# Where the weight ring and the activation buffers start in on-chip memory, modulo 256 bytes

## The chip, the cores and the metric

The kernel runs on one core of one Trainium2 chip. The metric is the device time of one launch in microseconds. The kernel before takes 2471.91 us, the median of 3 runs (2470.83 to 2474.18).

## The reference

A two-layer decoder trunk in float32 over 256 tokens with a model width of 2048. Cut to what matters:

```python
h = x                                         # (1, 256, 2048)
for i in range(2):
    xn = rmsnorm(h, g_mix[i])
    mix = attn_mixer(xn, ...) if i == 0 else rglru_mixer(xn, ...)   # projections 2048 -> 5656 / 4096, and back
    h = h + mix
    h = h + swiglu(rmsnorm(h, g_ffn[i]), wg, wu, wd)                # 2048 -> 2 x 5632 -> 2048
    gate = sigmoid(rmsnorm(h, g_ple[i]) @ w_ple_gate[i])            # 2048 -> 2048
    h = h + gate * (p[i] @ w_ple_proj[i])                           # 256 -> 2048
return rmsnorm(h, g_final)
```

Nearly all of the arithmetic is in these dense products of a (256 x K) activation with a (K x N) weight. There are about 443 MB of weights, and each is read once.

## The kernel before, in words

**Precision by splitting.** Every dense product is made of three products in the fast 32-bit matmul format. A weight is split into `w_hi` (the value rounded by a ScalarE copy, line 537) and `w_lo` (the rest, by VectorE, line 774). An activation is split into `x_hi` and `x_lo` in the same way. The product is `x_hi*w_hi + x_hi*w_lo + x_lo*w_hi`, on lines 1276, 1277 and 1278, all three into one PSUM accumulator.

**Slots.** The weights come in pieces of 2 k-tiles x 512 columns (512 KB), one DMA each, issued by SyncE. A piece is called a slot here. The ring has four places (`NRING = 4`): `raw` takes the DMA, `w_hi` and `w_lo` the two halves. Slot number t uses place t modulo 4. The whole program goes through 820 slots in one fixed order, phase after phase. TensorE does 12 matmuls for a slot: for each of 2 token tiles and each of 2 k-tiles the three products. In each of them the activation (128 x 128) is the stationary operand, which a weight load brings into the array, and the weight piece (128 x 512) is the moving operand. While one matmul streams its 512 columns, the weight load for the next matmul runs beside it. (Four slots are an exception, for the 24 gate columns: there the operands change roles.)

**Order.** Each engine runs its own list of instructions in an order fixed when the program is written; they meet through semaphores. ScalarE and VectorE prepare slot t+1 and later while TensorE multiplies slot t, as far as the ring lets them. Between slots TensorE does the transposes of results (line 1232) and, in the attention and recurrence phases, small plain float32 matmuls.

**Buffers.** The activations stand in three pairs of buffers, each with a `hi` and a `lo` part of [k-tiles, 256 tokens] in 4-byte elements: A (`xa_hi`, `xa_lo`, 16 k-tiles) feeds both products of the feed-forward block and the gate of the layer's end; B (`xb_hi`, `xb_lo`, 16 k-tiles) feeds the input and output projections of the mixers; H (`hid_hi`, `hid_lo`, 44 k-tiles) feeds the down projection and lies over B. A fourth pair, `pT_hi` and `pT_lo`, feeds one slot in nine of the last phase of each layer. One k-tile takes 1024 bytes per partition, and the second token tile begins 512 bytes behind the first, so every stationary operand of a buffer has the same start modulo 256. The same holds for the weights: the second k-tile in a place begins 2048 bytes behind the first.

**Addresses.** All buffers are laid out by hand, one behind the other from byte 16512 of the partition (`put`), and some at computed offsets (`at`). The distance of two ring places is `WROW * 4` bytes. From these lines follow the starts, modulo 256, in the table of the section on the change.

Of the kernel before, what the change touches and what calls it, by code (L numbers as in the profile page):

```python
# [27 lines left out]
F32R = mybir.dt.float32r  # L28
# [7 lines left out]
S = NT * P  # L36
D = 2048
KD = D // P
DFF = 5632
KF = DFF // P  # L40
CW = 512
# [16 lines left out]
LRU_C = 8.0  # L58
NBLK = 8
XPAD = 260  # L60
WROW = 2 * CW + 32


class Kind:
# [164 lines left out]
def trunk(nc, x, p, g_mix, g_ffn, g_ple, g_final, w_in_attn, cmp_pe_k, cmp_w1_k, cmp_w2_k,  # L229
# [6 lines left out]
    with ctx:  # L236

        base = (nc.sbuf_base + 63) // 64 * 64
        size = nc.sbuf_usable_end - 64 - base
        ctx.enter_context(nc.sbuf_tensor("slab", [P, size - 64], mybir.dt.uint8))  # L240
        top = [base]

        def at(name, shape, dt, offset):
            return nc.alloc_sbuf_tensor_at(name, [P, *shape], dt, offset=offset)

        def put(name, shape, dt=F32):
            n = int(np.prod(shape)) * (2 if dt == BF16 else 4)
            t = at(name, shape, dt, top[0])
            top[0] += (n + 31) // 32 * 32
            return t  # L250

        h = put("h", [NT, D])
        raw = put("raw", [NRING, 2 * CW])
        w_hi = put("w_hi", [NRING, WROW], F32R)
        w_lo = put("w_lo", [NRING, WROW], F32R)
        stage = put("stage", [NT, CW])
# [20 lines left out]
        ssqb = put("ssqb", [NT, HEADS])  # L277
        rstdb = put("rstdb", [NT, HEADS])
        sp_t = put("sp_t", [6, KD])
        a_off = top[0]  # L280
        big = a_off + 2 * KD * S * 4
        s_off = big + 2 * KD * S * 4
        assert big + 2 * KF * S * 4 <= base + size - 64, (big + 2 * KF * S * 4, base + size)
        X = {"A": (at("xa_hi", [KD, S], F32R, a_off), at("xa_lo", [KD, S], F32R, a_off + KD * S * 4)),
             "B": (at("xb_hi", [KD, S], F32R, big), at("xb_lo", [KD, S], F32R, big + KD * S * 4)),
             "H": (at("hid_hi", [KF, S], F32R, big), at("hid_lo", [KF, S], F32R, big + KF * S * 4))}

        vrow = at("vrow", [3, P], F32, s_off + 28672)
        gmix = at("gmix", [P], F32, s_off + 28672 + 3 * P * 4)
# [1278 lines left out]
```

How the kernel before makes its waits and increments, by code:

```python
            def load_slot(q, i, r, j):  # L423
                t = slot_no(q, i, r, j)
                s = ring_place(t, j)
                k0, nk, c0, w = slot_shape(q, r, j)
                if not (isinstance(t, int) and t < NRING):
                    sp.wait_ge(lo_ready, t - (NRING - 1))
                col = q.cols[r] + c0 + i * (CW if q.loop else 2 * CW)
                weight = q.weight[r].replace("gate", "proj") if is_proj(q, j) else q.weight[r]
                src = W[weight][:, k0:k0 + nk, bass.ds(col, w)]
                dst = raw[:, s, 0:nk * w].rearrange("p (k n) -> p k n", k=nk)
                sp.dma_start(dst, src).then_inc(raw_in[s], 16)
# [1 line left out]
            def load_vectors():  # L435
                sp.wait_ge(vrow_clear, 1)
                for dst, src in ((vrow[32:64, 0], g_ffn.rearrange("a (k p) -> (a k) p", p=P)),
                                 (vrow[64:96, 0], g_ple.rearrange("a (k p) -> (a k) p", p=P)),
                                 (vrow[96:104, 0], diff_subln[0]),
# [9 lines left out]
            def run_chunk(q, i, r, prev):  # L449
# [13 lines left out]
                        sp.dma_start(lam_in[:, n, :], v[0].partition_broadcast(P)).then_inc(lam_in_sem, 16)  # L463
                if q.name == "gkvc" and r == 1:
                    sp.wait_ge(vec_turned, 2)
                    sp.dma_start(w1[1][:], cmp_w1_v[0].rearrange("l d e -> d l e")).then_inc(w1_in[1], 16)
                if q.name == "out0" and i == 0 and r == 1:
                    sp.wait_ge(scored, 32)
                    for layer in range(2):
```

## Time and profile before

| what | value |
|---|---|
| time, median of 3 runs | 2471.91 us (2470.83 to 2474.18) |
| the profiled execution: its own time, and its span | 2473.23 us, 2471.5 us |
| mean granted TensorE clock | 0.997 |
| TensorE matmuls, busy | 2445.6 us, 99% |
| VectorE, ScalarE busy | 53%, 46% |
| DMA | 443.87 MB, 180 GB/s on average |

The span is from the first to the last instruction. The profiled execution's own time is 1.7 us longer than its span and 1.3 us longer than the median of the timed runs. The busy time of one matmul contains the passage through the array, which overlaps the next matmul's, so the cost of a matmul is not its duration (about 393 ns) but the distance from its start to the start of the next. That distance is read from the timeline, whose starts are given to 0.01 us; over a slot of 12 matmuls the rounding is below 1 ns for each.

### The profile page before, as it was taken

The page shows a single profiled execution, that of the slowest core. Times are in us where ns is not written, and L with a number is a line of the kernel's source. Part 1 is how long each engine was busy: PE and PEld are TensorE (multiplying, and loading weights), DVE is VectorE, ACT ScalarE, POOL GpSimd, SP SyncE. Part 2 cuts the span into 40 slices and gives each one's busy share as a digit, 9 for nine tenths or more (in the row PEclk, how much of TensorE's full clock was granted, in tenths as well). Part 3 has the DMA queues.
Part 4 walks back from the last instruction along what each step waited for, and adds up shares of the span by engine and source line. Part 5 has one row for each costly group of instructions (what it writes and reads, how often), then busy time and mean ns, then how long its engine had stood idle before and what let it go on. Part 6 is the DMA issues. An engine that isn't in the chain of part 4 may idle for free.

```text
span 2471.5 us, 29756 instructions
## 1 busy us (share of the span) xinstructions
PE 2445.6 (99%) x11084; PEld 1994.7 (81%) x11084; DVE 1315.4 (53%) x1677; ACT 1139.5 (46%) x1533; POOL 3.2 (0%) x17
## 2 busy tenths in 40 slices
PE   8999999999999999999999999999999999999997
PEld 7888778888888888888888888888888888888886
DVE  5545665555454454444566676554454454444455
ACT  5435555544444444444454575544444444344454
POOL 0000000000000000000000000000000000000000
PEclk9999999999999999999999999999999999999999
DMA  7744435666666665555557445566666666555563
GB/s 215 229 120 120 131 117 182 185 187 186 187 187 182 186 186 184 187 188 187 187 187 235 140 154 178 186 183 185 187 187 184 186 183 188 186 187 187 187 204 135
DMA packets 234042, 443.87 MB, mean 180 GB/s; under 512 B 16184, under 2 KB 21344, under 8 KB 233824
## 3 DMA queue, kind: packets, MB, share of 16 engines
q1 hardware_dynamic: 233904, 442.62, 58.7%
q8 instruction: 60, 0.98, 0.2%
q14 instruction: 30, 0.25, 0.0%
q10 hardware_dynamic: 48, 0.02, 0.0%
HBM read 440.49 MB, written 2.10 MB: 179 GB/s over the span
## 4 chain that ended last, share of the span: by engine, by line
PE 96%; DVE 1%; ACT 1%; DMA 1%; issue 0%; ACTq 0%; DVEq 0%
PE ps L1278 30%; PE ps L1276 30%; PE ps L1277 30%; PE ps L1232 2%; PE ps L1487 1%; PE ps L1400 1%; PE ps L1331 1%; DMA raw<-in_w_in_rec_dram 1%; DVE w_lo L774 0%; ACT w_hi L537 0%; PE ps L1412 0%; PE ps L1437 0%; ACT prob L691 0%; DMA h<-in_x_dram 0%; PE ps L1371 0%
## 5 line engine op out<-in xcount | busy, mean ns | idle before, releaser
L774 DVE TENSOR_TENSOR w_lo<-raw,w_hi 128x1024 fp32r<-128x1024 f32 x820 | 998.4, 1220 | 1071.1 <-ACT w_hi L537 1070.1
L537 ACT ACTIVATE w_hi<-raw 128x1024 fp32r<-128x1024 f32 x820 | 863.1, 1055 | 1137.3 <-PE ps L1278 1108.2
L1278 PE MATMUL ps<-w_hi,xa_lo 128*128 128x512 f32 x1664 | 656.9, 395 | 0.0
L1277 PE MATMUL ps<-w_lo,xa_hi 128*128 128x512 f32 x1664 | 654.2, 393 | 0.0
L1276 PE MATMUL ps<-w_hi,xa_hi 128*128 128x512 f32 x1664 | 653.9, 393 | 0.0
L1277 PEld LDWEIGHTS ps<-w_lo,xa_hi 128*128 128x128 f32 x1664 | 312.7, 188 | 73.1
L1276 PEld LDWEIGHTS ps<-w_hi,xa_hi 128*128 128x128 f32 x1664 | 312.6, 188 | 70.5
L1278 PEld LDWEIGHTS ps<-w_hi,xa_lo 128*128 128x128 f32 x1664 | 312.6, 188 | 68.8
L1276 PE MATMUL ps<-w_hi,xb_hi 128*128 128x512 f32 x864 | 351.3, 407 | 3.9 <-DVE xb_lo L837 2.3
L1278 PE MATMUL ps<-w_hi,xb_lo 128*128 128x512 f32 x864 | 341.9, 396 | 0.0
L1277 PE MATMUL ps<-w_lo,xb_hi 128*128 128x512 f32 x864 | 341.0, 395 | 0.0
L1278 PE MATMUL ps<-w_hi,hid_lo 128*128 128x512 f32 x704 | 277.9, 395 | 0.0
L1277 PE MATMUL ps<-w_lo,hid_hi 128*128 128x512 f32 x704 | 276.8, 393 | 0.0
L1276 PE MATMUL ps<-w_hi,hid_hi 128*128 128x512 f32 x704 | 276.3, 392 | 0.0
L1276 PEld LDWEIGHTS ps<-w_hi,xb_hi 128*128 128x128 f32 x864 | 163.2, 189 | 43.5 <-issue 4.5
L1278 PEld LDWEIGHTS ps<-w_hi,xb_lo 128*128 128x128 f32 x864 | 163.2, 189 | 37.0
L1277 PEld LDWEIGHTS ps<-w_lo,xb_hi 128*128 128x128 f32 x864 | 163.3, 189 | 35.1
L1277 PEld LDWEIGHTS ps<-w_lo,hid_hi 128*128 128x128 f32 x704 | 132.3, 188 | 31.1
L1276 PEld LDWEIGHTS ps<-w_hi,hid_hi 128*128 128x128 f32 x704 | 132.3, 188 | 30.0
L1278 PEld LDWEIGHTS ps<-w_hi,hid_lo 128*128 128x128 f32 x704 | 132.3, 188 | 29.1
L691 ACT ACTIVATE prob<-prob,nmax 128x128 f32<-128x128 f32 (+1 forms) x64 | 28.6, 448 | 56.0 <-DVE nmax L1058 56.0
L1232 PEld LDWEIGHTS ps<-ident,stage 128*128 128x128 f32 x304 | 35.5, 140 | 5.1
(200 smaller groups left out, 1043.9 us busy)
## 6 DMA issues: line engine op xcount, KB each, us to landing
raw<-in_w_ffn_gate_dram SPq DMA_DIRECT2D x176, 512.0 KB, 3.6
raw<-in_w_ffn_up_dram SPq DMA_DIRECT2D x176, 512.0 KB, 3.6
raw<-in_w_ffn_down_dram SPq DMA_DIRECT2D x176, 512.0 KB, 3.6
raw<-in_w_in_attn_dram SPq DMA_DIRECT2D x88, 512.0 KB, 3.7
raw<-in_w_ple_gate_dram SPq DMA_DIRECT2D x64, 512.0 KB, 3.8
raw<-in_w_in_rec_dram SPq DMA_DIRECT2D x64, 512.0 KB, 4.3
raw<-in_w_out_attn_dram SPq DMA_DIRECT2D x32, 512.0 KB, 3.7
raw<-in_w_out_rec_dram SPq DMA_DIRECT2D x32, 512.0 KB, 3.7
```

The costliest lines, as they stand in the source:

```text
L537: nc.scalar.activation(w_hi[:, s, 0:n], raw[:, s, 0:n], ACT.Copy).then_inc(hi_ready, 1)
L691: ins = nc.scalar.activation(pr, pr, ACT.Exp, scale=-1.0, bias=nmax[:, u % 2, n:n + 1], accum_out=esum[:, u % 2, n:n + 1])
L774: nc.vector.tensor_tensor(w_lo[:, s, 0:n], raw[:, s, 0:n], w_hi[:, s, 0:n].bitcast(F32), ALU.subtract).then_inc(lo_ready, 1)
L1232: ins = nc.tensor.transpose(o, src(m, f), ident[:])
L1276: nc.tensor.matmul(o, xh[:, k, tok], w_hi[:, s, wk], start=(k == 0), stop=False)
L1277: nc.tensor.matmul(o, xh[:, k, tok], w_lo[:, s, wk], start=False, stop=False)
L1278: ins = nc.tensor.matmul(o, xl[:, k, tok], w_hi[:, s, wk], start=False, stop=(k == nkt - 1))
L1331: ins = nc.tensor.matmul(ps[:, EX + kind, 0:2 * NCMP].rearrange("p (g n) -> p g n", g=2), w1[kind][:, l], x30, start=(l == 0), stop=(l == ...
L1400: ins = nc.tensor.matmul(ps[:, EX, cols], q_t[:, m * P:(m + 1) * P], k_t[:, 0:(m + 1) * P], start=True, stop=True)
L1487: ins = nc.tensor.matmul(ps[:, EX + g, e * S:(e + 1) * S], lru_w[:, g, n, k, e * P:(e + 1) * P], xc[:, 2 * n + k], start=(k == 0), stop=(k ...
```

## The change

It changes addresses and nothing else: the instructions of every engine, their order and their waits are the same. The distance of two ring places goes from 4224 to 4160 bytes (padding of 128 bytes to 64), the ring and buffer A are rounded up to a multiple of 256, B begins 32 bytes later, H where B would begin without these 32, and `hid_lo` leaves 128 bytes free behind `hid_hi`.

```diff
-WROW = 2 * CW + 32
+WROW = 2 * CW + 16
@@
         raw = put("raw", [NRING, 2 * CW])
+        top[0] = (top[0] + 255) // 256 * 256
         w_hi = put("w_hi", [NRING, WROW], F32R)
         w_lo = put("w_lo", [NRING, WROW], F32R)
@@
-        a_off = top[0]
-        big = a_off + 2 * KD * S * 4
+        a_off = (top[0] + 255) // 256 * 256
+        big = a_off + 2 * KD * S * 4 + 32
+        hid_off = big - 32
         s_off = big + 2 * KD * S * 4
-        assert big + 2 * KF * S * 4 <= base + size - 64, (big + 2 * KF * S * 4, base + size)
+        assert hid_off + 2 * KF * S * 4 + 128 <= base + size - 64, (hid_off + 2 * KF * S * 4, base + size)
         X = {"A": (at("xa_hi", [KD, S], F32R, a_off), at("xa_lo", [KD, S], F32R, a_off + KD * S * 4)),
              "B": (at("xb_hi", [KD, S], F32R, big), at("xb_lo", [KD, S], F32R, big + KD * S * 4)),
-             "H": (at("hid_hi", [KF, S], F32R, big), at("hid_lo", [KF, S], F32R, big + KF * S * 4))}
+             "H": (at("hid_hi", [KF, S], F32R, hid_off), at("hid_lo", [KF, S], F32R, hid_off + KF * S * 4 + 128))}
```

Starts modulo 256 bytes, worked out from the code:

| buffer | role in the 512-column matmuls | before | after |
|---|---|---|---|
| `w_hi`, `w_lo`, places 0, 1, 2, 3 | moving | 128, 0, 128, 0 | 0, 64, 128, 192 |
| `xa_hi`, `xa_lo` | stationary | 192, 192 | 0, 0 |
| `xb_hi`, `xb_lo` | stationary | 192, 192 | 32, 32 |
| `hid_hi`, `hid_lo` | stationary | 192, 192 | 0, 128 |
| `pT_hi`, `pT_lo` | stationary | 128, 128 | 0, 0 |
| `raw`, `h` | source of the split; residual | 128, 128 | 128, 128 |
| `stage`, `sg`, `ident` | results, identity for transposes | 128 | 0 |
| small tensors of the attention and the recurrence | | 192, 128 | 32, 0 |

## Rows read from the trace of the kernel before

**Rows 1.** The page, busy time (share of the span) and number of instructions.

```profile
PE 2445.6 (99%) x11084; PEld 1994.7 (81%) x11084; DVE 1315.4 (53%) x1677; ACT 1139.5 (46%) x1533; POOL 3.2 (0%) x17
```

**Rows 2.** The page, the span in 40 slices: TensorE busy and its granted clock.

```profile
PE   8999999999999999999999999999999999999997
PEclk9999999999999999999999999999999999999999
```

**Rows 3.** The page, costliest groups: busy us, mean ns; idle before, releaser.

```profile
L774 DVE TENSOR_TENSOR w_lo<-raw,w_hi 128x1024 fp32r<-128x1024 f32 x820 | 998.4, 1220 | 1071.1 <-ACT w_hi L537 1070.1
L537 ACT ACTIVATE w_hi<-raw 128x1024 fp32r<-128x1024 f32 x820 | 863.1, 1055 | 1137.3 <-PE ps L1278 1108.2
L1278 PE MATMUL ps<-w_hi,xa_lo 128*128 128x512 f32 x1664 | 656.9, 395 | 0.0
...
L1278 PE MATMUL ps<-w_hi,xb_lo 128*128 128x512 f32 x864 | 341.9, 396 | 0.0
...
L1278 PE MATMUL ps<-w_hi,hid_lo 128*128 128x512 f32 x704 | 277.9, 395 | 0.0
```

**Rows 4.** Waits of TensorE: us in total, times, longest.

```profile
PE ps L1494 <- DMA gmix<-in_g_mix_dram: 3.2, 1, 3.2
PE ps L1232 <- DVE xb_lo L837: 2.5, 1, 2.5
PE ps L1276 <- DVE xb_lo L837: 2.3, 1, 2.3
...
PE ps L1276 <- DVE w_lo L774: 0.6, 1, 0.6
```

**Rows 5.** Timeline of TensorE, down projection: an even slot, then an odd one.

```profile
1141.58 0.39 PE L1276 MATMUL ps<-w_hi,hid_hi 128*128 128x512 f32 x1
...
1142.04 0.40 PE L1278 MATMUL ps<-w_hi,hid_lo 128*128 128x512 f32 x1
...
1144.37 0.39 PE L1276 MATMUL ps<-w_hi,hid_hi 128*128 128x512 f32 x1
1144.60 0.39 PE L1277 MATMUL ps<-w_lo,hid_hi 128*128 128x512 f32 x1
...
1147.12 0.39 PE L1276 MATMUL ps<-w_hi,hid_hi 128*128 128x512 f32 x1
```

**Rows 6.** Timeline of TensorE, an even slot with `pT` stationary.

```profile
2380.75 0.39 PE L1276 MATMUL ps<-w_hi,pT_hi 128*128 128x512 f32 x1
...
2381.91 0.39 PE L1278 MATMUL ps<-w_hi,pT_lo 128*128 128x512 f32 x1
...
2383.49 0.39 PE L1276 MATMUL ps<-w_hi,xa_hi 128*128 128x512 f32 x1
```

**Rows 7.** Timeline of TensorE, an odd slot with `pT` stationary.

```profile
2405.65 0.39 PE L1276 MATMUL ps<-w_hi,pT_hi 128*128 128x512 f32 x1
2405.88 0.40 PE L1277 MATMUL ps<-w_lo,pT_hi 128*128 128x512 f32 x1
...
2408.45 0.39 PE L1276 MATMUL ps<-w_hi,xa_hi 128*128 128x512 f32 x1
```

**Rows 8.** The chain of waits in order of time, from 1368 us: start, us.

```profile
1368.60 3.45 PE ps L1487 x16
```

**Rows 9.** Instructions on `pT_hi`, and line 1232 by operand: ns min/median/max.

```profile
L1276 PE MATMUL ps<-w_hi,pT_hi x32: 389/392/398, 1226.5 to 2457.6; 128*128 128x512 f32 x32
...
L1232 PE MATMUL ps<-ident,stage x304: 271/273/275, 48.8 to 2122.2; 128*128 128x128 f32 x152
...
L1232 PE MATMUL ps<-ident,o_all x32: 270/272/273, 356.3 to 380.4; 128*128 128x128 f32 x32
```

## The prediction

> **What bounds the kernel now.** I read the page's busy times first: TensorE is busy for 99% of the span, VectorE for 53%, ScalarE for 46% [rows 1], and the slices show the granted clock at 2.4 GHz practically throughout, with no gap on TensorE behind the first slice [rows 2]. Then the waits of TensorE: the longest are 3.2, 2.5 and 2.3 us, once each, and weights that come late cost it 0.6 us in the whole run [rows 4]. ScalarE and VectorE are the ones that wait: 1108 us of ScalarE's idle time ahead of the splits ends with TensorE's release of a ring place, and VectorE waits for ScalarE [rows 3]. So the kernel's time is a number of matmuls by the distance of their starts. The dense ones, three lines with equal counts, are 3 x (1664 + 864 + 704) = 9696 [rows 3], and 3 x 32 = 96 with `pT` [rows 9], 9792 together.
>
> **The spacing depends on the place in the ring.** In the down projection an even slot takes from 1141.58 to 1144.37, 2.79 us for 12 matmuls or 232.5 ns each; the next, odd one takes until 1147.12, 2.75 us or 229.2 ns [rows 5]. Both do the same work on the same engine with nothing late. What differs is the address: the weights start at 128 modulo 256 in even places and at 0 in odd ones, the activations at 192 in both. The slots that multiply `pT` change the other operand, to 128. There the even slot takes 2.74 us, 228.3 ns each, and its last seven 1.58 us, 225.7 ns [rows 6]; the odd one takes 2.80 us, 233.3 ns [rows 7]. So even places take longer with activations at 192 and less with activations at 128. The place alone doesn't decide it, nor the activation alone; the simplest reading is that the distance of the moving operand's start from the stationary operand's, modulo 256, does, while a weight load runs beside the matmul.
>
> I call that distance the offset (weight start minus activation start, modulo 256). The trace then has one value for each of four:
> - offset 0: 228.3 ns over the whole slot; 225.7 once it has settled, seven matmuls [rows 6];
> - offset 64 (odd places now): 229.2; settled, 2.52 us for eleven, 229.1 [rows 5];
> - offset 128: 233.3; settled, 2.57 us for eleven, 233.6 [rows 7];
> - offset 192 (even places now): 232.5; settled, 2.33 us for ten, 233.0 [rows 5].
>
> The kernel now runs at offsets 64 and 192 by turns: (229.2 + 232.5)/2 = 230.85 ns whole, 231.05 settled. 9792 x 230.85 = 2260 us of the 2473.2 us of the profiled execution.
>
> The Trainium skill speaks against any effect: its page "TensorE: Matmul & The Clock Gate", section "Step-by-step: what each phase is for", says that TensorE has two independent read ports into SBUF and that loading the next weights takes no bandwidth from the running matmul. By that rule addresses don't matter and the change is worth nothing (it is the second rival below). The trace doesn't bear it out, with 229.2 against 232.5 ns in neighbouring slots.
>
> **The change, part by part.**
>
> *Buffer A, 3 x 1664 = 4992 matmuls.* With A at 0 and the places at 0, 64, 128 and 192, all four offsets come once in four slots. Whole slots: (228.3 + 229.2 + 233.3 + 232.5)/4 = 230.8, a change of 0.0 ns. Settled: (225.7 + 229.1 + 233.6 + 233.0)/4 = 230.35, a change of -0.7 ns. The truth depends on how long the low value at offset 0 takes to settle: in the `pT` slot it took five matmuls, but there the stationary base changed as well. The step from place 3 to place 0 is there after the change too, so some of it will be paid. I take -0.5 ns, nearer to the settled value, since nine of ten matmuls of the three other kinds of slot are settled ones. 4992 x -0.5 = -2.5 us.
>
> *Buffer H, 3 x 704 = 2112.* `hid_hi` at 0 and `hid_lo` at 128: two of three weight loads see the offset of the place, one that plus 128. Over four places each offset still comes equally often, so if the costs add, the mean is A's: 2112 x -0.5 = -1.1 us. Whether a mixed sequence settles at all is not in the trace; its bounds are the lowest and highest settled values, 225.7 and 233.6, so -5.3 to +2.6 ns against the present mean of 231.0: -11.2 to +5.5 us.
>
> *Buffer B, 3 x 864 = 2592.* At 32 the offsets become 224, 32, 96 and 160, halfway between those seen. No row shows one. Interpolating between neighbours gives the mean again, 2592 x -0.5 = -1.3 us, which I take. Bounds from the slots: 225.7 and 233.6, so -13.7 to +6.7 us. The rows farther off are the small matmuls of the recurrence, 16 of 256 columns in 3.45 us, 215.6 ns each, with both operands in 4-byte elements [rows 8]: if they are what a matmul costs without any disturbance and B came free of it, (215.6 - 231.0) x 2592 = -40 us. In the other direction, if a start off the 64-byte grid cost one more step of the size between offsets 0 and 128 (233.6 - 225.7 = 7.9 ns), it is +20.5 us.
>
> The Trainium skill's "SBUF — State Buffer", section "Specifications (TRN2)", gives 16-byte lines in SBUF; 32 is a multiple of that, so by this page a start at 32 touches no more lines than one at 0 and the +20.5 us would not arise. No run here shows the size of a line.
>
> *`pT`, 96 matmuls.* It now meets all offsets: nothing.
>
> *The splits.* ScalarE's copy takes 1055 ns and VectorE's subtraction 1220 ns per slot of about 2.77 us [rows 3]; both have over half of each slot to spare, so even 10% on either for a new address would stay hidden, and its cover is gone only beyond 2.7 us. *Transposes:* 273 ns with a source at 128 and 272 with one at 192 [rows 9]; they don't feel the address, 0. *The small matmuls* of attention and recurrence move from 192 to 32 or 0; they are about 200 us of the run together with the transposes, and 215.6 ns apart where their operands both stand at 192 [rows 8]; 0, at most a us or two either way.
>
> *Sum:* -2.5 - 1.1 - 1.3 = -4.9 us. From the profiled execution's 2473.2 that is 2468.3; the timed runs have their median 1.3 us lower, so 2467.0. If TensorE gets through a slot quicker, nothing is late next, as the splits have the slack just named and raw weights arrive well ahead.
>
> **The rivals.**
>
> *B and H land on the quick side.* The four values are not symmetric around a middle, and the states are plainly sequences that lock into a rhythm: 225.7 settled against 228.3 with the entry. An activation 32 bytes off may lock into the quick one in all places. Then B gains 5.3 ns: 2592 x -5.3 = -13.7, with -3.6 from A and H, -17.3: 2454.6 us. If H does the same, 2444.5. For it: the low value exists. Against it: it has been seen at one offset only.
>
> *Addresses shift the pattern, not the mean.* The disturbances are only moved about, and the entry into the low value eats its gain, as in the whole-slot values (0.0 ns): 2471.9 us. This is also what the skill's rule on the two read ports would give. For it: whole slots sum to 230.8 against 230.85. Against it: the `pT` slot's settled 225.7.
>
> *Slower: the 32-byte start of B.* If every weight load from B reaches over one more piece of memory and this delays the streaming weights by one step, B's matmuls rise by 7.9 ns: +20.5 - 3.6 = +16.9, 2488.8 us. It decides against the change as soon as B loses more than 3.6/2592 = 1.4 ns per matmul. For it: every start in the dense part is a multiple of 64 now, and half of those slots already take 232.5 ns. Against it: nothing in the rows shows the load as the limit. A milder form is that offset isn't the rule and 0 against 0 is a costly pairing; all at 233.6 would be 9792 x 2.6 = +25 us.
>
> **How the numbers follow.** What a measurement of this kernel can tell from no change is about 0.2%, 4.9 us. Forecast (offset rule), 0.38: its centre lies on that border, so 0.20 faster and 0.18 same; its own range 2461 to 2472. Quick side: 0.25, faster. Pattern only: 0.12, same. Slower: 0.25. That gives faster 0.45, same 0.30, slower 0.25. The range 2450 to 2482 holds the forecast, the second rival, most of B's quick side and the milder half of the slower one, and leaves out about 0.08 below and 0.11 above.
>
> **What would show it.** In the timeline after, the slots of the feed-forward phases in places 0, 1, 2, 3 should take about 2.72 to 2.74, 2.75, 2.80 and 2.79 us. If A's slots show these four, the offset rule holds; if place 0 takes 2.8, the absolute address counts. B's slots in the projections tell the 32-byte question: all near 2.71 is the first rival, all above 2.82 the slower one. Transposes and splits should keep their durations, and TensorE's waits their few us. The prediction is wrong if A's four slots average below 2.74 or above 2.79 us, or if B leaves the band of 225.7 to 233.6 ns.

## The result, and the profile after

The changed kernel takes 2481.76 us, the median of 5 runs (2481.38 to 2482.02), against 2472.92 us for the kernel before beside it. The ratio is 1.0035 with a 95% interval of 1.0021 to 1.0049: slower by 0.35%, some 9 us. The profiled execution spans 2480.1 us, 8.6 us more than before. The time lies within the range of 2450 to 2482 us, but only 0.2 us inside its upper end, and in the direction that had a chance of 0.25.

The page says that the kind of kernel is the same. TensorE is still busy 99% of the span, and the two groups that split the weights keep their durations:

```profile
PE 2454.5 (99%) x11084; PEld 1993.5 (80%) x11084; DVE 1315.5 (53%) x1677; ACT 1138.7 (46%) x1533; POOL 3.2 (0%) x17
...
L776 DVE TENSOR_TENSOR w_lo<-raw,w_hi 128x1024 fp32r<-128x1024 f32 x820 | 998.2, 1220 | 1080.4 <-ACT w_hi L539 1077.0
L539 ACT ACTIVATE w_hi<-raw 128x1024 fp32r<-128x1024 f32 x820 | 862.1, 1054 | 1147.7 <-PE ps L1280 1128.7
```

Line numbers have moved by two. VectorE takes 1220 ns and ScalarE 1054 against 1055 [rows 3]; both idle 9 to 10 us more, because TensorE hands the ring places back later. The waits of TensorE (total us, times, longest) are again a few us, the largest at the very start:

```profile
PE ps L1496 <- DMA gmix<-in_g_mix_dram: 5.0, 1, 5.0
PE ps L1234 <- DVE xb_lo L839: 2.5, 1, 2.5
PE ps L1278 <- DVE xb_lo L839: 2.3, 1, 2.3
```

Against [rows 4] the first is 1.8 us longer, a DMA before the first matmul. The transposes (ns min/median/max) are as in [rows 9], 273 and 272 ns, though `ident` and `o_all` have moved:

```profile
L1234 PE MATMUL ps<-ident,stage x304: 270/273/273, 49.7 to 2129.0; 128*128 128x128 f32 x152
...
L1234 PE MATMUL ps<-ident,o_all x32: 270/272/273, 358.7 to 381.7; 128*128 128x128 f32 x32
```

So the time is in the distance between dense matmuls. The timeline of TensorE gives it slot by slot (12 matmuls between the rows shown). Four slots of the feed-forward phase with buffer A, places 1, 2, 3 and 0:

```profile
701.90 0.40 PE L1278 MATMUL ps<-w_hi,xa_hi 128*128 128x512 f32 x1
...
704.66 0.40 PE L1278 MATMUL ps<-w_hi,xa_hi 128*128 128x512 f32 x1
...
707.46 0.39 PE L1278 MATMUL ps<-w_hi,xa_hi 128*128 128x512 f32 x1
...
710.25 0.39 PE L1278 MATMUL ps<-w_hi,xa_hi 128*128 128x512 f32 x1
...
713.00 0.40 PE L1278 MATMUL ps<-w_hi,xa_hi 128*128 128x512 f32 x1
```

They take 2.76, 2.80, 2.79 and 2.75 us. Offset 0 is the short one and 128 and 192 are the long ones, as the offset rule had it. Now buffer B (places 0 to 3, the last row is a transpose) and buffer H (places 0 to 3):

```profile
436.77 0.40 PE L1278 MATMUL ps<-w_hi,xb_hi 128*128 128x512 f32 x1
...
439.57 0.40 PE L1278 MATMUL ps<-w_hi,xb_hi 128*128 128x512 f32 x1
...
442.37 0.40 PE L1278 MATMUL ps<-w_hi,xb_hi 128*128 128x512 f32 x1
...
445.18 0.39 PE L1278 MATMUL ps<-w_hi,xb_hi 128*128 128x512 f32 x1
...
447.98 0.27 PE L1234 MATMUL ps<-ident,h 128*128 128x128 f32 x1
...
1139.92 0.40 PE L1278 MATMUL ps<-w_hi,hid_hi 128*128 128x512 f32 x1
...
1142.72 0.39 PE L1278 MATMUL ps<-w_hi,hid_hi 128*128 128x512 f32 x1
...
1145.51 0.39 PE L1278 MATMUL ps<-w_hi,hid_hi 128*128 128x512 f32 x1
...
1148.31 0.39 PE L1278 MATMUL ps<-w_hi,hid_hi 128*128 128x512 f32 x1
...
1151.09 0.40 PE L1278 MATMUL ps<-w_hi,hid_hi 128*128 128x512 f32 x1
```

B takes 2.80 to 2.81 us in every place, H 2.78 to 2.80. No short slot is left in either, where before every other slot took 2.75 [rows 5].

The same over the whole trace: mean distance in ns from one dense matmul's start to the next, distances of 300 ns and more left out (they contain other work), about 9600 distances:

| | before | after | after, by place 0, 1, 2, 3 |
|---|---|---|---|
| A | 230.9 | 231.1 | 228.3, 230.3, 232.9, 233.0 |
| B | 231.1 | 233.4 | 233.3, 233.3, 233.5, 233.5 |
| H | 230.9 | 232.6 | 232.7, 233.0, 233.1, 231.6 |

With all distances counted, long ones too, A gives 1.2 us more, B 3.4 (its short distances alone 2.25 ns x 2465 = 5.5, its long ones 2 less), H 3.6 and `pT` nothing, 8.2 together. The other matmuls give 1.5 less and the start 1.8 more; that is the 8.6 us of the span, to rounding.

The 2 us less in B's long distances are no gain of the change. In the profiled execution of the kernel before, the granted clock fell to half, 1.2 GHz, for 3.4 us in the attention phase, behind a stretch in which TensorE was busy for 1.6 of 3.9 us; seven of B's matmuls stand 427 ns apart there. In that of the changed kernel it did not fall there. The same stretch before and after, with the granted clock in the third column from the end:

```profile
359.90:363.40 3.50, 3.50 (x10) 2.67 (x10) 2.85 (x5) 0.00 (x0) 0.00 (x0) 0.51 0.63 206
```

```profile
360.00:363.50 3.50, 1.50 (x7) 1.26 (x8) 3.50 (x6) 1.85 (x4) 0.00 (x0) 1.00 0.34 115
```

With the matmuls of the first slot, also 427 ns apart, it is 13 such distances before and 8 after, 1.0 us; one distance of 1.03 us before, behind weights that came late, makes most of the rest. So B's loss by the addresses is nearer to the 5.5 us of its short distances than to 3.4.

### The profile page after: what moved, and what is told of

The parts are those of the page before. It is cut to its first block, busy times and chain, and to the rows that moved or that the text cites. A ratio compares the mean times of both kernels' runs of the same rounds, so it can differ in the third digit from the quotient of the medians.

```text
span 2480.1 us, 29756 instructions
## 1 busy us (share of the span) xinstructions
PE 2454.5 (99%) x11084; PEld 1993.5 (80%) x11084; DVE 1315.5 (53%) x1677; ACT 1138.7 (46%) x1533; POOL 3.2 (0%) x17
## 4 chain that ended last, share of the span: by engine, by line
PE 98%; DVE 1%; ACT 0%; DMA 0%; issue 0%; ACTq 0%; DVEq 0%
PE ps L1278 31%; PE ps L1280 30%; PE ps L1279 30%; PE ps L1234 2%; PE ps L1489 1%; PE ps L1402 1%; PE ps L1333 1%; PE ps L1414 0%; PE ps L1439 0%; PE ps L1440 0%; PE ps L1441 0%; DMA h<-in_x_dram 0%; PE ps L1373 0%; PE ps L1363 0%; PE ps L1352 0%
## 5 line engine op out<-in xcount | busy, mean ns | idle before, releaser
L776 DVE TENSOR_TENSOR w_lo<-raw,w_hi 128x1024 fp32r<-128x1024 f32 x820 | 998.2, 1220 | 1080.4 <-ACT w_hi L539 1077.0
L539 ACT ACTIVATE w_hi<-raw 128x1024 fp32r<-128x1024 f32 x820 | 862.1, 1054 | 1147.7 <-PE ps L1280 1128.7
```

The lines of the kernel that those rows point to most:

```text
L539: nc.scalar.activation(w_hi[:, s, 0:n], raw[:, s, 0:n], ACT.Copy).then_inc(hi_ready, 1)
L776: nc.vector.tensor_tensor(w_lo[:, s, 0:n], raw[:, s, 0:n], w_hi[:, s, 0:n].bitcast(F32), ALU.subtract).then_inc(lo_ready, 1)
```

## The experiments

All of them build on the changed kernel. "Offset" is the start of the moving weights minus the start of the stationary activations, modulo 256 bytes. A spacing without a row is a mean over the run's trace, formed as in the table above.

**Everything at one residue** (4 runs). "Residue" is the start modulo 256. The edit against the changed kernel, cut to what matters:

```diff
-WROW = 2 * CW + 16
+WROW = 2 * CW + 0
@@
-        big = a_off + 2 * KD * S * 4 + 32
-        hid_off = big - 32
+        big = a_off - 0 + 2 * KD * S * 4 + 0
+        hid_off = a_off - 0 + 2 * KD * S * 4 + 0
```

and `hid_lo` directly behind `hid_hi`.

> All ring places, A, B, H and pT start at 0 modulo 256 (ring step 4096 bytes), so every 512-column matmul runs at offset 0 (weight start minus activation start, modulo 256). Theory 1, the offset rule: every slot settles at the low value seen in place 0 of the changed kernel, 226.7 ns instead of a mean of 232.0; 9792 x -5.3 = -52 us against the changed kernel, about 2430 us. Rival: the low value needs a change of place, or the other engines that now read and write at the same residue disturb it: spacing of 229 or more, 2455 us or more.

Measured: 2432.57 us (2432.27 to 2432.84), ratio to the kernel before 0.9838, interval 0.9822 to 0.9855. The timeline with A:

```profile
700.73 0.39 PE L1278 MATMUL ps<-w_hi,xa_hi 128*128 128x512 f32 x1
...
703.45 0.39 PE L1278 MATMUL ps<-w_hi,xa_hi 128*128 128x512 f32 x1
...
706.17 0.39 PE L1278 MATMUL ps<-w_hi,xa_hi 128*128 128x512 f32 x1
```

Each slot takes 2.72 us, 226.7 ns per matmul, in all four places; over the trace A has 226.8, H 226.7, B 227.7. The expectation of about 2430 us was met. It is a version that beats both kernels, by 40 us and 49 us, and needs less memory than either. The low value needs no change of place, and there is no sign that engines working at the same residue get into each other's way (`raw` and `h` stay at 128).

**B back at 0** (10 runs): `big` without the 32 bytes, all else as changed.

> The changed kernel with buffer B at 0 instead of 32 modulo 256; all else as changed (places at 0, 64, 128, 192). Theory 1: B's slots become like A's, 228.3, 230.3, 232.9, 233.0 by place, mean 231.1 instead of 233.4; 2592 x -2.3 = -6 us against the changed kernel, 2476 us. Rival (B is slow because it is interleaved with other work and has other neighbours, not because of the 32 bytes): B stays at 233.4, 2482 us.

Measured: 2475.10 us (2474.71 to 2477.43), 6.7 us below the changed kernel; ratio to before 1.0013 (1.0004 to 1.0023). B's mean is 231.2 ns, and B's matmuls give about 6 us of the difference. Its place 0 takes 2.74 us where it took 2.80:

```profile
433.11 0.39 PE L1278 MATMUL ps<-w_hi,xb_hi 128*128 128x512 f32 x1
...
435.85 0.40 PE L1278 MATMUL ps<-w_hi,xb_hi 128*128 128x512 f32 x1
```

A and H kept their values to 0.1 ns in every place. B's loss comes from the 32 bytes, not from its neighbours.

**`hid_lo` back at 0** (one run): without the 128 bytes between `hid_hi` and `hid_lo`.

> The changed kernel with hid_lo at 0 instead of 128 modulo 256, like hid_hi. Theory 1: H's slots become like A's, mean 231.1 instead of 232.6 (place 0 at 228.3); 2112 x -1.5 = -3 us against the changed kernel. Rival (H's cost has nothing to do with hi and lo standing apart): place 0 of H stays at 232.7.

Measured: 2478.74 us in one run, 3.0 below the changed kernel. H has A's values by place (228.6, 230.3, 232.8, 233.0), place 0:

```profile
1149.81 0.39 PE L1278 MATMUL ps<-w_hi,hid_hi 128*128 128x512 f32 x1
...
1152.55 0.40 PE L1278 MATMUL ps<-w_hi,hid_hi 128*128 128x512 f32 x1
```

That is 2.74 us against 2.80. H's matmuls give 3.0 us. The time of one run could not show as little by itself, since the runs of the kernel before lie up to 4 us apart; the spacing shows it. A's place 0 settles at 227 ns after five matmuls. In H's place 0 of the changed kernel the distances are 236, 232, 233, 236, 224, 231, 236, 235, 233, 233, 235 and 231 ns: with the offset jumping by 128 at every third weight load, twelve matmuls don't settle.

**The rotation alone** (10 runs): both edits together.

> The changed kernel with B and hid_lo both at 0: only the ring's rotation (0, 64, 128, 192) and the common start of all activations are left of the change. Theory 1: every buffer has A's values by place (228.3, 230.3, 232.9, 233.0, mean 231.1), against 230.9 before; 9792 x 0.2 = 2 us over before, 2472 to 2475 us, so B's and H's new starts account for the rest of the change's loss. Rival: B's and H's losses don't add up, and 3 us or more of the loss stay (2476 us or above).

Measured: 2473.48 us (2471.81 to 2475.01), ratio 1.0002 (0.9993 to 1.0012), no difference to the kernel before. A has 231.1, B 231.2, H 231.2 ns. The losses of B and H add up: 2481.8 - 6.7 - 3.0 = 2472.1. What is left of the change, four offsets by turns in place of two, is worth nothing that the time shows. (By the spacing, 0.1 to 0.3 ns above before, it costs up to 2 us, which is less than the runs' own spread.)

**Three odd multiples of 32** (one run): all places at 0, A at 32, B at 96, H at 160.

> All ring places at 0; A at 32 (offset 224), B at 96 (offset 160), H at 160 (offset 96). Every buffer has one offset, so settled values can be read for three odd multiples of 32. Theory 1a (a stationary start off the 64-byte grid costs by itself): all three at 233 or above. Theory 1b (the cost is a smooth function of the offset): 224 between 226.7 and 233, 96 between 229 and 233.6, 160 at about 233.

Measured: 2496.37 us. A (offset 224):

```profile
705.76 0.40 PE L1278 MATMUL ps<-w_hi,xa_hi 128*128 128x512 f32 x1
...
708.56 0.40 PE L1278 MATMUL ps<-w_hi,xa_hi 128*128 128x512 f32 x1
```

2.80 us, 233.3 ns, and the same for H at offset 96; B at 160 has 234.1. The smooth function of 1b fails at 224, which is 32 bytes from the best value and costs the full 6.6 ns; 96 and 160 it had about right. 1a fits here, but it names the wrong cause, as the next run shows.

**Both operands off the grid** (one run): places and A at 32, B at 64, H at 0.

> All ring places at 32, A at 32 (offset 0), B at 64 (offset 224), H at 0 (offset 32). Theory 1 (the offset decides, not the absolute start): A at 226.7 although both operands start off the 64-byte grid, B at 233 to 234 although its stationary operand is on the grid. Rival (a start off the 64-byte grid costs by itself): A above 230.

Measured: 2463.86 us. A, then H:

```profile
700.85 0.39 PE L1278 MATMUL ps<-w_hi,xa_hi 128*128 128x512 f32 x1
...
703.57 0.39 PE L1278 MATMUL ps<-w_hi,xa_hi 128*128 128x512 f32 x1
...
1140.44 0.40 PE L1278 MATMUL ps<-w_hi,hid_hi 128*128 128x512 f32 x1
...
1143.24 0.40 PE L1278 MATMUL ps<-w_hi,hid_hi 128*128 128x512 f32 x1
```

A: 2.72 us with both operands 32 bytes off the 64-byte grid. H: 2.80 us with its stationary operand at 0 and the weights at 32. B at offset 224 has 233.2 with its stationary operand on the grid. Theory 1a is out: at offsets 0 and 224 the offset decides, not where either operand starts.

**Finer steps** (one run each): ring steps of 4112 and of 4100 bytes, so that the places stand 16 or 4 bytes apart.

> Ring step 4112 bytes, so the places start at 0, 16, 32 and 48 modulo 256; A at 0 (offsets 0, 16, 32, 48), B at 128 (offsets 128 to 176), H at 192 (offsets 64 to 112). It reads the spacing at twelve offsets in one trace. Theory 1 (offset 0 is one of few low values, everything off the 64-byte grid costs 233): 226.7 to 228 in A's place 0, 233 in its places 1 to 3, H 229 in place 0 and 233 in 1 to 3, B 233 or more; time about 2480 us or more. Rival (a smooth valley around 0): A's place 1 lies between 226.7 and 229.

> Ring step 4100 bytes, places at 0, 4, 8 and 12 modulo 256; A at 0 (offsets 0, 4, 8, 12), B at 64 (192 to 204), H at 32 (224 to 236). Theory 1 (memory is reached in pieces larger than 12 bytes, and a start inside a piece costs one more): A at 233 in places 1 to 3 and 228 in place 0. Rival (only larger distances matter): A stays near 227 in all four places.

Measured 2481.61 and 2489.74 us. Mean distance in ns by ring place, A and H only (a slot's first matmuls still carry the place before, which can change a mean by over 1 ns: offset 0 has 228.8 behind offset 12, as shown, and 230.0 behind offset 48):

| offset | 0 | 4 | 8 | 12 | 16 | 32 | 48 | 64 | 80 | 96 | 112 | 224 | 228 | 232 | 236 |
|---|---|---|---|---|---|---|---|---|---|---|---|---|---|---|---|
| ns | 228.8 | 237.5 | 233.1 | 230.5 | 231.5 | 233.7 | 232.7 | 229.1 | 231.1 | 234.3 | 231.1 | 232.8 | 235.9 | 234.1 | 228.9 |

The worst of them was 4 bytes from the best. B, left out of the table because other work stands between its slots, has 237.8 at offset 196, again 4 bytes past a multiple of 64. These rows are A in place 1 of the second run, 2.84 us:

```profile
703.58 0.40 PE L1279 MATMUL ps<-w_hi,xa_hi 128*128 128x512 f32 x1
...
706.42 0.40 PE L1279 MATMUL ps<-w_hi,xa_hi 128*128 128x512 f32 x1
```

Theory 1 of the first run had H's place 0, A's places 2 and 3 and the time about right and missed the other places of A and H: 16, 80 and 112 lie well below 233, and so do 12 and 236 of the second run, so "off the 64-byte grid costs 233" is wrong. Its rival missed too, with 231.5 at offset 16, and both theories of the second run missed, so there is no valley around 0 either. No settled sequence was found below 226.7.

The first run also shows a limit of the offset rule. B's place 0 has offset 128 with the same starts each time, and still two different sequences. In some slots distances of 229 and 238 ns alternate, 2.80 us for twelve, 233.3 ns each (first two rows). In others a pattern of seven repeats, 1.63 us for seven, 232.4 ns each (last two rows):

```profile
411.95 0.39 PE L1279 MATMUL ps<-w_hi,xb_hi 128*128 128x512 f32 x1
...
414.75 0.39 PE L1279 MATMUL ps<-w_hi,xb_hi 128*128 128x512 f32 x1
...
1311.21 0.39 PE L1279 MATMUL ps<-w_hi,xb_hi 128*128 128x512 f32 x1
...
1312.84 0.39 PE L1280 MATMUL ps<-w_lo,xb_hi 128*128 128x512 f32 x1
```

So the offset alone doesn't fix the spacing to the last nanosecond; what ran just before seems to choose the sequence, which was not tested.

**Is it the length of the weight load?** Three runs with stationary operands of 32 columns instead of 128: for the middle product alone, on the changed kernel; for all products, at offset 0; and for all at the offsets of the scan by 32 (both times with 128 columns kept in a product's first and last k-tile). The edit of the first:

```diff
-                        nc.tensor.matmul(o, xh[:, k, tok], w_lo[:, s, wk], start=False, stop=False)
+                        nc.tensor.matmul(o[0:32], xh[:, k, m * P:m * P + 32], w_lo[:, s, wk], start=False, stop=False)
```

> The changed kernel with the x_hi*w_lo product cut to 32 stationary columns (rows 0 to 31 of the output only, the low product of the other 96 tokens of each tile is left out). The weight load for it, which runs beside the first of each three matmuls, becomes short (about 100 ns instead of 188); all matmuls still stream 512 columns. Theory 1 (the excess over about 216 ns comes from the weight load's reads beside the stream): the distance from the first matmul's start to the second's falls by 6 ns or more, the other two keep 230 to 233. Rival (the stream costs this by itself, by its own start address): all three keep their spacing.

The loads (ns min/median/max) did become short:

```profile
L1278 PEld LDWEIGHTS ps<-w_hi,xa_hi x1664: 187/188/190, 457.8 to 2453.9; 128*128 128x128 f32 x185
...
L1279 PEld LDWEIGHTS ps<-w_lo,xa_hi x1664: 107/108/112, 458.0 to 2454.1; 128*32 128x32 f32 x185
```

In A the distance beside the short load fell by 1.6 ns, from 231.2 to 229.6, where theory 1 wanted 6, and the one after the third matmul rose from 231.0 to 232.0. The means of A, B and H fell by 0.3, 1.3 and 1.7 ns. The time was 2472.48 us, 9.3 below the changed kernel.

> Everything at 0 modulo 256 (offset 0 throughout), and the three products cut to 32 stationary columns in all but the first and last k-tile (output rows 32 to 127 miss most of the sum). Weight loads take about 108 ns instead of 188, the streams keep 512 columns. Theory 2 (the excess over 216 ns grows with the reads of the weight load): the settled spacing falls from 226.7 to about 219. Rival, theory 3 (only the start of the load beside the stream counts, or a fixed cost of the stream): it stays at 226.7 within 1 ns.

> The same short loads with A at offset 224, B at 160, H at 96, where full loads settle at 233.3 ns. Theory 2: A and H fall by 6 ns or more. Theory 3: they stay at 233.3. If they fall to the spacing of the same loads at offset 0, the address only matters through the part of the load that was cut.

Measured 2473.61 and 2508.52 us. H at offset 0 with short loads, then A at offset 224 with short loads:

```profile
1142.73 0.40 PE L1280 MATMUL ps<-w_hi,hid_hi 128*32 128x512 f32 x1
...
1145.51 0.40 PE L1280 MATMUL ps<-w_hi,hid_hi 128*32 128x512 f32 x1
```

```profile
703.22 0.40 PE L1280 MATMUL ps<-w_hi,xa_hi 128*32 128x512 f32 x1
...
706.10 0.40 PE L1280 MATMUL ps<-w_hi,xa_hi 128*32 128x512 f32 x1
```

2.78 us (231.7 ns) where full loads take 226.7, and 2.88 us (240 ns) where they take 233.3. The 2.88 us are the more frequent of A's values, others are 2.78 and 2.81; A's mean over the trace is 237.9. H at offset 96 stayed at 233.2, and B at 160 fell from 234.1 to 231.1. Theories 2 and 3 both fail: in these two runs less to load made the matmuls farther apart in two cases, left one as it was and helped one. A load of 32 columns starts where the full one does and covers 384 bytes less, so neither its first reads alone nor its amount alone sets the spacing. But these edits also cut the rows of the output that a matmul writes from 128 to 32, and no run separates that from the load. How the two streams get in each other's way stays open.

**Do the other engines take part?** (one run): everything at 0, splits cut to 64 columns.

> Everything at 0 modulo 256, and ScalarE's and VectorE's splits cut to 64 of 1024 columns from slot 16 on (the rest of each ring place keeps old values), so these engines hardly touch memory in the feed-forward phases. Theory 1 (the spacing is a matter between the two operands of TensorE alone): 226.7 ns unchanged in A and H. Rival (part of what is left over 216 ns comes from the other engines' traffic): a fall by 2 ns or more.

```profile
L540 ACT ACTIVATE w_hi<-raw 128x64 fp32r<-128x64 f32 (+1 forms) x820 | 222.1, 272 | 1682.8 <-PE ps L1282 1661.0 <-DMA raw<-in_w_in_attn_dram 12.8 <-DMA raw<-in_w_in_rec_dram 8.7
```

ScalarE's split falls from a mean of 1056 to 272 ns, and A stays at 226.8 and H at 226.7. The run took 2429.16 us, 3.4 less than with full splits, none of it from A and H (2.5 of it between B's matmuls).

The DMAs still ran here, but the last slots of a trace answer for them: no weights are left to fetch. With everything at 0, three of the last four slots fill this stretch (the last two numbers are the DMA engines' busy share and GB/s), and the first of them takes the usual 2.72 us:

```profile
2407.08:2415.24 8.16, 8.16 (x38) 6.76 (x36) 1.23 (x1) 1.08 (x2) 0.00 (x0) 1.00 0.01 2
```

```profile
2407.08 0.39 PE L1278 MATMUL ps<-w_hi,xa_hi 128*128 128x512 f32 x1
...
2409.80 0.39 PE L1278 MATMUL ps<-w_hi,xa_hi 128*128 128x512 f32 x1
```

In the kernel before, the same slots still take 2.78, 2.76 and 2.78 us by turns with the DMA engines 1% busy. So neither ScalarE and VectorE nor the DMAs take part; the spacing is a matter of TensorE's own operands.

## Why the prediction was wrong

*What bounds the kernel, and the offset as the cause:* right. TensorE alone sets the time, splits and transposes kept their durations, and the offset decides (both operands moved by 32 bytes together: no change; one alone: 226.7 to 233.3), up to the choice between two sequences that offset 128 shows. Neither of the signs of being wrong that the prediction named came up: A's four slots average 2.77 us, and B's 233.4 ns stay in the band. They were too wide to tell a gain of 5 us from a loss of 9.

*Buffer A:* the whole-slot values read from two `pT` slots and two slots of the down projection were 228.3, 229.2, 233.3 and 232.5; measured 228.3, 230.3, 232.9 and 233.0. The step "I take -0.5 ns, nearer to the settled value" was mis-sized: it was +0.3 ns, +1.2 us in place of -2.5. The entry was paid in full, five matmuls in place 0 as in the `pT` slot, and another 1 ns in place 1. The sum over whole slots, 0.0, was the better number, and rows 6 showed the entry. The settled 225.7 was 1 ns too low besides: seven matmuls read to 0.01 us leave an error of over 1 ns, and the settled value is 226.7.

*Buffer H:* "if the costs add, the mean is A's" failed. They don't add: three products with two offsets run at 232.6, the same with one offset at 231.2. +1.7 ns against -0.5, +3.6 us against -1.1, inside the bounds given.

*Buffer B:* "Interpolating between neighbours gives the mean again" is the step that failed most, +2.3 ns against -0.5. Between 0 and 64 lies not 228 but 233, and all four of B's new offsets sit at the high level. In time it is +5.5 us in the short distances, in place of -1.3; the bound of +6.7 us from the rows held it. The slower rival named the 32-byte start of B, and its break-even of 1.4 ns was passed, but its mechanism (a start off the grid costs a step of 7.9 ns) is refuted: 2.3 ns, and it was the offset.

*The signs:* the three errors all went one way, and three small gains of 1 to 3 us were three losses of 1 to 6. That the time still fell within the range is luck: its upper end was drawn for the milder half of a slower rival whose mechanism is refuted.

The rule of the Trainium skill, "TensorE: Matmul & The Clock Gate", section "Step-by-step: what each phase is for", that the next weight load takes nothing from the running matmul was rightly set aside. Between the residues of the first experiment and the changed kernel's lie 49 us. What the rule says of bandwidth no run here shows.

## What to carry to other kernels

Where TensorE alternates weight loads with 512-column matmuls in 4-byte elements, read the distance between starts slot by slot. If it depends on the buffer place and on nothing else, look at the start addresses modulo 256 and let moving and stationary operands start at the same residue, in all places and all operands of a sequence; here that was worth 40 us of 2472. A padding that spreads buffers over residues averages good and bad pairings. Do not interpolate between measured offsets: 226.7 and 237.5 ns were found 4 bytes apart, and one run with one residue per buffer reads off several offsets at once.

## What the hardware showed that was not expected

The settled sequences repeat, to the 1 ns of the trace, and add up to whole multiples of 6.67 ns, which is 16 cycles of the granted 2.4 GHz: 226.7 (34 of them) at offset 0; 225.8 + 229.2 + 231.7 = 686.7 (103) at 64; 233.3 (35) at 192 in the changed kernel, and 231 and 236 by turns, 466.7 together (70), at the same offset in the kernel before; and at 128 either the pattern of seven that sums to 1626.7 (244) or 229 and 238 by turns, again 466.7 together. This was seen, and what keeps the beat was not tested.

The lowest spacing found for a 512-column matmul, 226.7 ns, is still 11 above the 215.6 of [rows 8], which are matmuls of 256 columns in plain float32. Neither the other engines' traffic nor a shorter load brought it down.
